# Y corrected ahead of the key products, keys scaled by ScalarE, the decay table read in place, one score matmul over key blocks

## What is computed

```python
# gated delta rule, 8 heads of 128, forward and reverse; g = cumulated log decay
lmat = where(strict, beta[:, None] * (k @ k.T) * decay, 0) + eye
t_inv = triangular_solve(lmat, eye)          # one per chunk, head, direction
v_new = t_inv @ (beta * v) - (t_inv @ (beta * exp(g) * k)) @ state
o     = (q * exp(g)) @ state + ((q @ k.T) * decay) @ v_new
state = state * exp(g_last) + (k * exp(g_last - g)).T @ v_new
# windowed attention, 16 query heads on 4 key heads of 64, |i - j| <= 128
s = q @ k_band.T * 64 ** -0.5 ; p = softmax([s, sink])[:-1] ; o = p @ v_band
```

## Time and profile before

| | us |
|---|---|
| median of three runs (2341.98 to 2345.06) | 2342.47 |
| profiled execution, its own time | 2347.63 |
| its span | 2345.8 |
| TensorE busy | 2261.1 (96%) |
| GpSimd busy | 1142.9 (49%) |
| VectorE busy | 1113.9 (47%) |
| ScalarE busy | 833.2 (36%) |
| mean granted TensorE clock | 0.987 |

### The profile page before, as it was taken

How to read it: one execution, slowest core, us unless ns; L and a number is a source line. 1 busy time by engine, 2 the same in 40 slices (tenths; PEclk the granted TensorE clock), 3 DMA queues, 4 the chain that set the end, 5 groups by cost and what they waited for, 6 DMA issues and landing times.

```text
span 2345.8 us, 34138 instructions
## 1 busy us (share of the span) xinstructions
PE 2261.1 (96%) x13464; PEld 1823.5 (78%) x13464; DVE 1113.9 (47%) x1948; ACT 833.2 (36%) x2220; POOL 1142.9 (49%) x674
## 2 busy tenths in 40 slices
PE   8999999999999899999999999999899999999997
PEld 6777877877777788888777778778677787888885
DVE  4677677764444611110256776777544466111003
ACT  3555445466641211110135454444665403111100
POOL 5453333324337466666544442332343375666664
PEclk9999999999999999999999999999999999999998
DMA  4221111111124223322222211211111332322322
GB/s 152 72 81 48 48 57 57 43 50 46 55 79 143 75 91 98 99 92 97 92 99 72 81 47 41 64 51 51 41 55 55 108 108 90 99 92 97 117 90 81
DMA packets 53886, 182.64 MB, mean 78 GB/s; under 512 B 7520, under 2 KB 8160, under 8 KB 53728
## 3 DMA queue, kind: packets, MB, share of 16 engines
q1 hardware_dynamic: 48976, 167.01, 22.1%
q10 hardware_dynamic: 4752, 13.45, 1.6%
HBM read 169.94 MB, written 4.19 MB: 74 GB/s over the span
## 4 chain that ended last, share of the span: by engine, by line
PE 86%; DVE 9%; issue 2%; ACT 2%; DMA 1%; POOL 0%; DVEq 0%; ACTq 0%; POOLq 0%
PE PS L586 19%; PE PS L588 18%; PE PS L587 18%; PE PS L754 11%; PE PS L844 2%; PE PS L958 2%; PE PS L1025 2%; PE PS L830 2%; PE PS L972 1%; PE PS L848 1%; PE PS L903 1%; PE PS L887 1%; PE PS L781 1%; PE PS L894 1%; PE PS L924 1%
## 5 line engine op out<-in xcount | busy, mean ns | idle before, releaser
L547 POOL TENSOR_SCALAR wh<-w_raw 128x1024 fp32r<-128x1024 f32 (+1 forms) x255 | 277.1, 1087 | 1029.5 <-DMA w_raw<-stream 1028.6
L550 POOL TENSOR_TENSOR wl<-w_raw,wh 128x1024 fp32r<-128x1024 f32 (+1 forms) x255 | 615.5, 2414 | 21.3
L586 PE MATMUL PS<-xh,wh 128*128 128x512 f32 x992 | 398.2, 401 | 11.1 <-issue 6.1
L588 PE MATMUL PS<-xl,wh 128*128 128x512 f32 x992 | 390.3, 393 | 0.0
L587 PE MATMUL PS<-xh,wl 128*128 128x512 f32 x992 | 389.2, 392 | 0.0
L586 PEld LDWEIGHTS PS<-xh,wh 128*128 128x128 f32 x992 | 188.2, 190 | 57.3 <-issue 12.7
L588 PEld LDWEIGHTS PS<-xl,wh 128*128 128x128 f32 x992 | 187.7, 189 | 40.6
L587 PEld LDWEIGHTS PS<-xh,wl 128*128 128x128 f32 x992 | 188.6, 190 | 37.4
L754 PE MATMUL PS<-xh,wh 128*128 128x512 f32 x448 | 205.3, 458 | 5.1 <-DVEq L1692 3.4
L2000 DVE TENSOR_TENSOR hf<-sg,PS 128x512 f32<-128x512 f32 x44 | 30.3, 688 | 355.5 <-PE PS L588 355.5
L1645 DVE SCALAR_TENSOR_TENSOR conv_acc<-PS,cw,conv_acc 128x510 f32<-128x510 f32 x192 | 143.9, 749 | 105.3 <-ACT conv_acc L1187 99.8
(11 more groups left out here) (293 smaller groups left out, 4779.3 us busy)
## 6 DMA issues: line engine op xcount, KB each, us to landing
w_raw<-stream SPq DMA_DIRECT2D x254, 512.0 KB, 3.4
w_raw_spare<-stream SPq DMA_DIRECT2D x46, 512.0 KB, 3.5
x<-x_in ACTq DMA_DIRECT2D x6, 512.0 KB, 7.0
qx<-qx SPq DMA_DIRECT2D x48, 64.0 KB, 2.0
raw<-raw SPq DMA_DIRECT2D x32, 64.0 KB, 2.2
ln_g<-ln_rows ACTq DMA_DIRECT2D x4, 512.0 KB, 4.0
ln_b<-ln_rows ACTq DMA_DIRECT2D x4, 512.0 KB, 5.0
x_park<-x ACTq DMA_DIRECT2D x4, 512.0 KB, 5.0
```

The costliest lines, as they stand in the source:

```text
L547: nc.gpsimd.tensor_scalar(wh[s][:, w], w_raw[s][:, w], 1.0, 1.0, ALU.mult, ALU.mult).then_inc(w_hi_done, 1)
L550: nc.gpsimd.tensor_tensor(wl[s][:, w], w_raw[s][:, w], wh[s][:, w].bitcast(F32), ALU.subtract).then_inc(split_done, 1)
L586: mm(o, ah, bh, start=first, stop=False)
L588: return mm(o, ah, bl, start=False, stop=last)
```

## The change

VectorE corrects Y (`YF`) before it makes `kb` and the scaled `kn`, and its `fill_out` behind level 6 moves behind both. `front_scale` is gone. ScalarE makes the next head's `kn` with `scale_keys`, two chunks behind level 3 and two behind level 5; for a layer's first head all four behind i = 10. `ht` is gone, and its readers index `tab`. `score` issues one matmul over all key blocks of a query block.

```diff
--- before.py
+++ after.py
@@ -243,7 +243,6 @@
         kb = head_buf("kb", [P, CHUNKS - 1, P])
         O1 = [head_buf(f"O1{r}", [P, P]) for r in range(2)]
         OT = [head_buf(f"OT{r}", [P, P]) for r in range(2)]
-        ht = [head_buf(f"ht{s}", [P, 5, 2, CHUNKS]) for s in range(2)]
         egl = [[head_buf(f"egl{s}{r}", [P, CHUNKS]) for r in range(2)] for s in range(2)]
         bdl = [head_buf(f"bdl{r}", [P, CHUNKS]) for r in range(2)]
         assert work[0] <= big + 110 * KB
@@ -359,7 +358,6 @@
         cum_zero = sem("cum_zero")
         gate_dve = sem("gate_dve")
         gate_act = sem("gate_act")
-        head_cols = sem("head_cols")
         k_normed = sem("k_normed")
         k_turned = sem("k_turned")
         kT_ready = sem("kT_ready")
@@ -952,12 +950,10 @@
                     g, b = divmod(n, CHUNKS)
                     lo, hi = max(b - 1, 0), min(b + 2, CHUNKS)
                     for t in range(2):
-                        for j in range(hi - lo):
-                            for half in range(2):
-                                part = slice(half * HD, (half + 1) * HD)
-                                mm(PS[:, half * 2 + t, j * P:(j + 1) * P], qx[part, g * 2 + t, b * P:(b + 1) * P],
-                                   kz[part, g, (lo + j) * P:(lo + j + 1) * P], start=j == 0, stop=lo + j == b,
-                                   skip_group_check=True)
+                        for half in range(2):
+                            part = slice(half * HD, (half + 1) * HD)
+                            mm(PS[:, half * 2 + t, 0:(hi - lo) * P], qx[part, g * 2 + t, b * P:(b + 1) * P],
+                               kz[part, g, lo * P:hi * P], start=True, stop=False, skip_group_check=True)
                     for j in range(hi - lo):
                         if lo + j == b:
                             continue
@@ -1207,6 +1203,12 @@
                                    PS[:, 2 + s, :]).then_inc(tok_stored, 1)
                 copy = nc.scalar.copy
 
+                def scale_keys(h, t, chunks):
+                    for c in chunks:
+                        ins = A(kn[t][:, c, :], raw[:, h + HEADS, c, :], ACT.Copy, scale=rn[:, h + HEADS, c:c + 1])
+                    if c == CHUNKS - 1:
+                        ins.then_inc(k_normed, 1)
+
                 def front_turned(m, t):
                     act.wait_ge(k_turned, m + 1)
                     copy(flat(kT[t][:]), PS[:, 5, :]).then_inc(kT_ready, 1)
@@ -1219,7 +1221,7 @@
                         A(egl[t][r][:], PS[:, 4 + r, :].rearrange("p (c t) -> p c t", c=CHUNKS)[:, :, edge], ACT.Exp)
                         for c in range(CHUNKS):
                             ins = A(DT[r][:, c, :], PS[:, 4 + r, c * P:(c + 1) * P], ACT.Exp,
-                                    bias=ht[t][:, T_NEG_CUM, r, c:c + 1])
+                                    bias=tab[:, m % HEADS, T_NEG_CUM, r, c:c + 1])
                         ins.then_inc(decay_done, 1)
 
                 def front_high(m):
@@ -1248,6 +1250,8 @@
                     if i == 9:
                         key_norms()
                     if i == 10:
+                        act.wait_ge(gate_dve, l * 19 + 19)
+                        scale_keys(0, 0, range(CHUNKS))
                         front_turned(l * HEADS, 0)
                 for s in range(2):
                     keep_tokens(U_QKV // 2 - 1, s, False)
@@ -1274,6 +1278,8 @@
                                 ins.then_inc(x_upd[r], 1)
                             else:
                                 copy(X[r][:].rearrange("p c t -> p (c t)"), PS[:, 3 * r + 2, :]).then_inc(x_upd[r], 1)
+                        if more and lev in (3, 5):
+                            scale_keys(h + 1, 1 - s, (0, 1) if lev == 3 else (2, 3))
                         if lev % 2 == 0:
                             fill_out(ISSUED[h, f"L{lev}"])
                         if not more and lev == 1:
@@ -1306,7 +1312,7 @@
                                 c = chunk[r]
                                 act.wait_ge(qs_mm[r], n * 3 + step)
                                 A(O1[r][:], PS[:, 2 + r, 0:P], ACT.Copy,
-                                  scale=ht[s][:, T_EG, r, c:c + 1]).then_inc(o1_ready[r], 1)
+                                  scale=tab[:, h, T_EG, r, c:c + 1]).then_inc(o1_ready[r], 1)
                         if step == 1:
                             if more:
                                 front_decays(n + 1, 1 - s, (0,))
@@ -1577,14 +1583,9 @@
                 def bank(b):
                     return PS[:, b, :].rearrange("p (c t) -> p c t", c=CHUNKS)
 
-                def front_scale(h, m, t):
-                    nc.vector.tensor_copy(ht[t][:].rearrange("p k r c -> p (k r c)"),
-                                          tab[:, bass.ds(h, 1)].rearrange("p a k r c -> p (a k r c)")).then_inc(head_cols, 1)
-                    TT(kn[t][:], raw[:, h + HEADS, :, :], cols(rn[:, h + HEADS, :]), ALU.mult).then_inc(k_normed, 1)
-
                 def front_beta(m, t, r):
                     dve.wait_ge(decay_done, m * 2 + r + 1)
-                    TT(TMP[r][:], DT[r][:], cols(ht[t][:, T_NEG_BETA, r, :]), ALU.mult).then_inc(beta_decay, 1)
+                    TT(TMP[r][:], DT[r][:], cols(tab[:, m % HEADS, T_NEG_BETA, r, :]), ALU.mult).then_inc(beta_decay, 1)
 
                 def front_nat(m, t, r):
 
@@ -1626,10 +1627,10 @@
                             dve.wait_ge(kb_ready[0], m + 1)
                         TT(to, kn[t][:, of, :], cols(bdl[r][:, of]), ALU.mult).then_inc(kb_ready[r], 1)
 
-                def edge_scales(t):
+                def edge_scales(h):
                     for r in range(2):
                         edge = P - 1 if r == 0 else 0
-                        TT(bdl[r][:], DT[r][:, :, edge], ht[t][:, T_BETA, r, :], ALU.mult).then_inc(bdl_done, 1)
+                        TT(bdl[r][:], DT[r][:, :, edge], tab[:, h, T_BETA, r, :], ALU.mult).then_inc(bdl_done, 1)
 
                 def conv_pair(i, sides=(0, 1)):
                     for s in sides:
@@ -1665,7 +1666,6 @@
                         split_sums()
                     if i == 9:
                         key_scales()
-                        front_scale(0, m0, 0)
                 for r in range(2):
                     front_nat(m0, 0, r)
                     front_sign(m0, r)
@@ -1742,7 +1742,7 @@
                             else:
                                 nc.vector.tensor_copy(Y[r][:], bank(3 * r + 1)).then_inc(y_upd[r], 1)
                         if lev == 4:
-                            edge_scales(s)
+                            edge_scales(h)
                         if lev in (3, 5):
                             fill_out(ISSUED[h, f"L{lev - 1}"])
                         if not more and lev == 1:
@@ -1755,19 +1755,17 @@
                             dve.wait_ge(rno_dve, l * 6 + 2)
                             TT(rno[:, 0:HEADS - 1, :], rno[:, 0:HEADS - 1, :], rn[:, 0:HEADS - 1, :],
                                ALU.mult).then_inc(rno_dve, 1)
-                    if more:
-                        front_scale(h + 1, n + 1, 1 - s)
-                    fill_out(ISSUED[h, "L6"])
-                    scaled_keys(n, s)
                     for r in range(2):
                         dve.wait_ge(y_fix[r], n + 1)
                         STT(YF[r][:], bank(3 * r), 1.0 / E_SCALE, Y[r][:], ALU.mult, ALU.add).then_inc(y_done[r], 1)
+                    scaled_keys(n, s)
+                    fill_out(ISSUED[h, "L6"])
                     for step in range(CHUNKS):
                         for r in range(2):
                             c = step if r == 0 else CHUNKS - 1 - step
                             if step > 0:
                                 dve.wait_ge(ks_mm[r], n * 3 + step)
-                                STT(R[r][:], PS[:, r, 0:P], ht[s][:, T_NEG_EG, r, c:c + 1], value(c), ALU.mult,
+                                STT(R[r][:], PS[:, r, 0:P], tab[:, h, T_NEG_EG, r, c:c + 1], value(c), ALU.mult,
                                     ALU.add).then_inc(r_ready[r], 1)
                         if step > 0:
                             output(step - 1)
```

## The result

| | before | changed kernel |
|---|---|---|
| median of all its runs | 2345.06 us (5 runs, 2341.98 to 2348.28) | 2358.73 us (5 runs, 2355.96 to 2364.19) |
| ratio to before, 95% interval | | 1.0063 [1.0049, 1.0076] |
| profiled execution: time, span | 2347.63, 2345.8 us | 2364.19, 2362.4 us |
| mean granted clock of TensorE | 0.987 | 0.984 |

The change costs 13.7 us on the medians (the ratio makes it 14.8, with 11.5 to 17.8 as its interval). The two profiled executions lie 16.6 us apart; the changed kernel's is the slowest of its five.

A forecast was written before the change was run, and what follows sets the result against it. It took TensorE, busy for 96% of the span, to bound the kernel. 11.0 + 4.0 + 2.4 - 3.9 - 1.5 = +12.0 us on the median of 2342.47 gave 2354.5 us, range 2346 to 2362.

The forecast's parts named there:

- first head's keys, two holes: Front part, each layer: key transposition waits 5.5 us for ScalarE's scaling behind the SiLU of tile 21; +11.0 us.
- low clock behind them: TensorE's matmuls behind each hole run at the lower clock level; 2.0 us for each layer, +4.0 us.
- key products behind YF, head 3: Head 3 of either layer: state product waits 1.2 us for kn, held up on VectorE by a GpSimd subtraction; +2.4 us.
- YF corrected first: The scan's first product in a head: its three waits for YF in the run all go; -3.9 us.
- wide score matmuls: Scores: cost goes with the columns, so wide matmuls save only some nanoseconds per instruction; -1.5 us.
- scaling in the levels, table in place: Behind levels 3 and 5 ScalarE's scalings fit its idle time; table operands keep their shape; nothing.
- The second rival: The wait at the first head's keys comes, but 5 of the 11.0 us are given back; 2345.5 us, chance 0.05.
- the third: The levels have no room on ScalarE: 28 pairs of scalings at 0.3 us, +8; 2362.5 us, chance 0.07.
- the fourth: Wide score matmuls are much cheaper per column, gaining 7.9 us instead of 1.5; 2348.1 us, chance 0.04.
- the first: The first head's key transposition does not wait for ScalarE, so only the gains stay; 2337.1 us, chance 0.04.

The follow-up runs named there:

- experiment 3: The kernel before with only the wide score matmuls, one over all key blocks; 2346.94 us, ratio 1.0008.
- experiment 5: The changed kernel with ScalarE scaling the first head's keys ahead of tile 21's centre tap instead of behind its SiLU; 2346.09 us, ratio 0.9999.
- e1: The changed kernel, but VectorE scales a layer's first head's keys behind tile 19, as in the kernel before; 2345.14 us, ratio 1.0000.
- e10: The same kernel as e1, timed again beside e9; 2344.62 us, ratio 0.9995 to the kernel before.
- e4: The kernel before with only YF moved ahead of the key products on VectorE; 2344.97 us, ratio 0.9997.
- e8: The kernel before with only the key products (kb, scaled kn) moved to ScalarE for all heads but the last; 2342.45 us, ratio 0.9985.
- e6: e1 with the key products (kb, scaled kn) moved from VectorE to ScalarE for all heads but the last; 2341.20 us, ratio 0.9980.
- e9: The same kernel as e6, timed again beside e10; 2343.52 us, ratio 0.9992 to the kernel before.
- e2: The kernel before with only the first head's keys scaled by ScalarE behind the SiLU of tile 21; 2361.46 us, ratio 1.0066.

## Why the prediction was right

It said 2354.5 us, slower; 2358.73 was measured, inside the range. Its +12.0 us stands against 13.7 by the medians. Of the 4.2 us between forecast and result 2.6 are the start: the median of three runs of before was 2342.47, that of five is 2345.06.

| step of the sum | forecast | measured in the changed kernel's trace |
|---|---|---|
| first head's keys, two holes | +11.0 | +10.96 (2 x 5.48) |
| low clock behind them | +4.0 | +3.9 (2.1 + 1.8) |
| key products behind YF, head 3 | +2.4 | +2.3 (1.02 + 1.29) |
| YF corrected first | -3.9 | -3.8, all three waits gone |
| wide score matmuls | -1.5 | -1.2 |
| scaling in the levels, table in place | 0 | no wait seen |
| sum | +12.0 | +12.2 |

The largest term was right because it was read off ScalarE's queue: in order, behind a SiLU whose start the trace of before already showed. Nothing gave the hole back. By starts, the changed kernel runs 4.8 us late at the first transposition (it was 0.7 early ahead of it), 8.0 us late at the scan of head 0 and 7.7 at that of head 7, 6.9 late ahead of the second hole and 14.3 behind it. The second rival is out. So are the third (the X copies, above), the fourth (experiment 3) and the first, which experiment 5 had to build.

The kn term was right by laying GpSimd's rows beside the new place. That was partly luck: GpSimd's starts depend on its transfers, which move with everything. At other places they did move, and I had not foreseen it. In layer 0 of the changed kernel, where the front part ends, VectorE and GpSimd:

```profile
169.71 4.21 DVE L1588 TENSOR_TENSOR TMP<-DT,tab 128x512 f32<-128x512 f32 x2
...
177.68 2.75 DVE L1600 COPY_PREDICATED NAT<-cst,minus_id 128x512 f32<-128x512 int32 x1
...
170.68 2.70 POOL L548 TENSOR_TENSOR wl<-w_raw,wh 128x1024 fp32r<-128x1024 f32 x1
...
177.44 2.38 POOL L548 TENSOR_TENSOR wl<-w_raw,wh 128x1024 fp32r<-128x1024 f32 x1
```

The predicated copy takes 2.75 us here (2.11 in before; 0.73 undisturbed). TensorE starts its next transposition (line 786) 1.24 us behind its last matmul there, against 0.62 us in before, so 0.6 us of this wait is new. And in layer 1 between heads 3 and 4 it waits 2.6 us on V, with a granted clock of 0.61 behind it (TensorE's row, then the stretch):

```profile
1537.44 0.40 PE L842 MATMUL PS<-V,X 128*128 128x128 f16 x4 [2.46 <-DVE V L1735]
```

```profile
1538.00:1542.00 4.00, 4.00 (x32) 3.29 (x30) 1.91 (x4) 1.76 (x4) 3.31 (x2) 0.61 0.02 4
```

That wait stood only in layer 0 before. Behind it the changed kernel is up to 20.7 us late by starts (at the scan of head 4); at the end it is 16.6 us late, so some 4 us come back, 1.5 of them at YF in head 5 and the others at places that the change does not touch. The 12.2 us of the table and the 16.6 between the two profiled executions therefore differ by several gains and losses of 0.3 to 3 us, and the table does not list them all. The wait on V in layer 1 does not need the hole or the YF order: e3, which changes the scores alone, has it in its trace, and so have e1 and e10, which are no slower than before; e4 and e8 have not. In the changed kernel VectorE's product for X there (1532.63, ahead of V) took 2.62 us instead of 0.41, beside a GpSimd subtraction that had started 0.4 us earlier. Why GpSimd meets it in some kernels and not in others is not shown.

What stays open: 13.7 to 14.8 us by the medians and the ratio, against 12.2 by the table, is within the interval (11.5 to 17.8). The hole with its low clock makes 14.9 in the table, and experiments 1 and 2 put 14.8 and 15.5 on it. The rest of the change should then have gained 2.7, and the intervals of the two timings of that kernel, e1 (2.6 us less to 2.6 more than before) and e10 (3.3 less to 0.9 more), do not settle whether it did.

## What to carry to other kernels

Before moving work to an idle engine, read what stands ahead of it in that engine's queue and what that waits for: ScalarE was idle for 64% of this kernel and still 5.5 us late, because its idle time was spent in front of an instruction that the moved work did not need. One place earlier in the queue, the same instructions were free. And an edit that removes a wait by moving an instruction back must be priced with the wait that this instruction may then bring; here -3.8 and +2.3 made nothing that the time could tell.

## What the runs showed of the hardware

**The time scatters with the time at the low clock.** e6 and e9 are the same kernel. Their profiled spans are 2334.4 and 2339.8 us, their times at the low clock 30.7 and 41.0: 5.4 us more span for 10.3 us more at half the clock, 0.52 us for each. The Trainium skill ("TensorE: Matmul & The Clock Gate", "Terms") puts the penalty at the throttled time multiplied by the share of pulses withheld, one half here; these two executions agree. The many executions of before say the same: of the 75 that were timed beside the experiments, the 19 with a mean granted clock of 0.990 have a mean span of 2340.3 us, the 6 with 0.986 one of 2348.4. Which comes first, a wait or the low clock behind it, the times do not tell. Across kernels the order is only roughly kept (changed kernel 61.4 and 2362.4, before 47.8 and 2345.8, e1 37.5 and 2342.5, but e8 47.8 and 2341.6). Single profiles of this kernel can thus differ by 2 to 5 us that no edit made.

**Each hole of TensorE cost 1.3 to 1.4 times its length:** 5.48 us idle and, over the four holes of the changed kernel and e2, 1.8 to 2.3 us at the low clock behind it. Filling it with matmuls that nobody needs brought the clock back to 1.00 without making the wait any shorter.

**Meeting a GpSimd instruction made 0.57 us into 2.56 on VectorE**, and the loss travels with the instruction: ahead of YF it delayed YF, behind YF it delayed the state product. Three ACTIVATEs of 128x128 with a scale take 0.99 us, more than the 0.57 of the undisturbed VectorE product, and were the better choice here because they always took it: on ScalarE all 28 such triples of e6 took 0.99 us, while the 16 products kn on VectorE have a mean of 0.785 in e1, with two of them long enough to hold up TensorE.
